# Third expert matrix read with four adjoining rows per partition, in a two-layer encoder step

## Chip, cores and metric

One Trainium2 chip, one core. The metric is the device time of one execution in microseconds, the median of several runs. The profile is one further execution, taken by the hardware profiler.

## The reference, cut to what matters

Two layers, each with a mixer and a mixture of experts. 256 prompt tokens and 128 sample tokens go through, all in float32. The part of concern is the experts' hidden layer, for each of 16 experts in each of two layers:

```python
for e in range(N_EXPERTS):                      # 16
    hdn = jax.nn.silu(t @ w1[e]) * (t @ w3[e])  # t: tokens x 1024; w1, w3: 1024 x 512
    y = y + gates[:, e:e + 1] * (hdn @ w2[e])   # w2: 512 x 1024
```

Each token goes to two experts (top-1 group, top-2 in it). The sum over the 512 inner values in `hdn @ w2[e]` may be taken in any order, as long as value and row belong together.

## The kernel before, in words

Each layer's experts are 16 steps of one pipeline. A step gathers up to 72 (layer 0) or 64 (layer 1) rows of its expert, turns them by TensorE, multiplies them with w1 and w3, takes silu and the product, turns the 512 inner values so that they lie along the partitions (four slices of 128), and multiplies them with w2. Each 2 MB matrix is a tile of 128 partitions x 4096 words. For accuracy, ScalarE writes a rounded copy of it (`moe_split_h`, line 1105, `moe_wh`) and VectorE the remainder (`moe_split_l`, line 1110, into `raw_lo` or `moe_wl`); TensorE uses both parts of the weights and of the data (lines 189 and 195, in layer 1 also 1384 to 1388).

SyncE issues the loads (line 777), three for each expert, in the order w1 of e, w3 of e, w2 of e-1, into six slots that are used in turn. A load waits on `w_used`, until TensorE is done with the matrix that held its slot six loads before; so SyncE runs ahead by what the slots allow. GpSimd loads the gathered rows (line 882), ScalarE's queue stores each expert's output (line 1159).

w1 and w3 are read with eight adjoining rows per partition ("o (p k) n"): 8 x 2 KB = 16 KB of one piece for each partition. w2 is read with rows 128 apart ("o (k p) n"): slice k of partition p is row 128 k + p, four runs of 4 KB each. So the inner values are turned in four contiguous slices of 128 columns. There are two forms of that:

- Layer 0, `transpose_hidden`, line 1402: for each expert four transposes of `hid` (72 rows x 128 columns as the stationary operand, which TensorE loads first; the identity moves). They stand in TensorE's order between the expert's successor's w1 product and its w3 product.
- Layer 1, `fold_hidden`, line 1431: the 128 output rows of w1's and w3's products hold two halves that must be added. A product with `fold` (two identities stacked) turns and adds at once: eight products for each expert, 128x128 stationary from `sil_all` or `hid_all`, 64 columns moving. The machine runs each of these float32 products as two weight loads and two matmuls, so 16 pairs. ScalarE's silu of the turned values (line 1186) and VectorE's `hidden_turned` (lines 1280 to 1284) wait for them, and then the w2 product.

Layer 0 has 72 columns of room for each expert and the plain form, layer 1 has 64 and the folding form. A third place that turns (line 1529) belongs to blocks for experts with more tokens than room; the profile shows no instruction of it.

`by_slice(x, n)` (line 919) views a row of n x 128 words as n slices, slice k being the columns k, k+n, k+2n and so on. VectorE uses it in `weigh_rows` (line 928), with n = 8, to bring the token rows into the order of w1's and w3's rows.

Of the kernel before, what the change touches and what calls it, by code (L numbers as in the profile page):

```python
# [29 lines left out]
P = 128  # L30
# [18 lines left out]
KE = DE // P  # L49
# [5 lines left out]
CAP = max(CAPS)  # L55
# [48 lines left out]
def build(nc, A, O):  # L104

    top = ExitStack()
    with top:
# [21 lines left out]
        ps = top.enter_context(nc.psum_tensor("ps", [P, 8, 512], F32))  # L129
# [548 lines left out]
        sil, hid = sil_all[0:CAP], hid_all[0:CAP]  # L678
# [6 lines left out]
        fold = gain[:, 0:CAPS[1]]  # L685
# [43 lines left out]
        BX, BA, BB, BH, BY, BR = 0, 2, 3, 4, 5, 7  # L729
# [21 lines left out]
        def at_least(eng, s, n):  # L751

            if not isinstance(n, int) or n > 0:
                eng.wait_ge(s, n)
# [7 lines left out]

        def w_in_expert(l, name, e):
            w = A[name][l, bass.ds(e, 1)]
            return w.rearrange("o (k p) n -> p (o k) n" if name == "moe_w2" else "o (p k) n -> p (o k) n", p=P)

        def moe_w_view(w, nk):
            return w.rearrange("p (k n) -> p k n", k=nk)


        def moe_sync(sp, l):
            m0, E0, S = M_MOE[l], NE * l, SLOT[l]

            def load(name, e, j, slot):
                if not (isinstance(j, int) and j < 6):
                    sp.wait_ge(w_used, m0 + j - 5)
                sp.dma_start(moe_w_view(w_raw[slot], KE if name == "moe_w2" else KD),
                             w_in_expert(l, name, e)).then_inc(raw_loaded[slot], 16)
# [42 lines left out]
            with sp.If(n_over > 0):  # L821
                with sp.Fori(0, EXTRA) as i:
                    e = sp.value_load(ovt_i[0:1, bass.ds(i, 1)], min_val=0, max_val=NE - 1)
                    row = sp.value_load(ovt_i[0:1, bass.ds(i + EXTRA, 1)], min_val=0, max_val=SLOTS)
                    sp.wait_ge(y_stored, 16 * (E0 + SENT if l else NE))
                    sp.wait_ge(w_used, m0 + 3 * NE)
                    if l:
                        sp.wait_ge(spread, TILES)
                    at_least(sp, s["st"], 16 * i + 16)
                    sp.dma_start(rows[0:cap, 0, :], xrows[bass.ds(row, cap), :]).then_inc(s["x"], 16)  # L830
                    for slot, name in enumerate(("moe_w1", "moe_w3", "moe_w2")):
                        sp.dma_start(moe_w_view(raw[:, slot, :], KE if slot == 2 else KD),
                                     w_in_expert(l, name, e)).then_inc(s["w"], 16)
                    at_least(sp, s["act"], 5 * i + 5)
                    sp.dma_start(yrows[bass.ds(row, cap), :], rows[0:cap, 2, :]).then_inc(s["st"], 16)
                sp.wait_ge(s["st"], 16 * EXTRA + 16)
# [82 lines left out]
        def by_slice(x, n):  # L919

            return x.rearrange("q (p k) -> q k p", k=n)
# [196 lines left out]
        def turned(i):  # L1118
            n = KE * CAPS[1]
            return ps[:, BH, n * i:n * (i + 1)].rearrange("p (k t) -> p k t", k=KE)  # L1120
# [247 lines left out]
        def moe_tensor(pe, l):  # L1368
# [29 lines left out]
            def transpose_hidden(e):  # L1398
                pe.wait_ge(hid_done, E0 + e + 1)
                at_least(pe, hl_ready, E0 + e)  # L1400
                for k in range(KE):
                    last = nc.tensor.transpose(ps[:, BH, k * CAP:(k + 1) * CAP], hid[:, k * P:(k + 1) * P],
                                               ident[0:CAP, 0:CAP])
                last.then_inc(hT_done, 1)

# [20 lines left out]
            def fold_hidden(e):  # L1426

                pe.wait_ge(halves, 2 * e + 2)
                for i, x in enumerate((sil_all, hid_all)):
                    for k in range(KE):  # L1430
                        last = nc.tensor.matmul(turned(i)[:, k], x[:, k * P:(k + 1) * P], fold, start=True, stop=True)
                last.then_inc(hT_done, 1)

            def folding_step(e, par, m):
                f = is_first(e)
                pe.wait_ge(xl_ready, E0 + e + 1)
                if not f:
                    pe.wait_ge(halves, 2 * e - 1)
                product_x(e, par, *([0, 0, 0] if f else [3 * e - 1, 2, 2 if par else 5]), BA).then_inc(w_used, 1)
                if not f:  # L1440
                    pe.wait_ge(halves, 2 * e)
                product_x(e, par, *([1, 1, 1] if f else [3 * e, 0, 3 if par else 0]), BB).then_inc(w_used, 1)
                if f:
                    gather_x(1)
                elif is_last(e):
                    turn_kept(1)
                elif not is_second(e):
                    transpose_x(e + 1, 1 - par)
                if not f:
                    product_y(e - 1, 3 * e + 1, 1, 4 if par else 1)  # L1450
                fold_hidden(e)
                if is_second(e):
                    transpose_x(2, 0)

            def step(e, par, m):
                f = is_first(e)
                pe.wait_ge(xl_ready, E0 + e + 1)
                at_least(pe, silu_done, E0 + e)
                product_x(e, par, *([0, 0, 0] if f else [3 * e - 1, 2, 2 if par else 5]), BA).then_inc(w_used, 1)
                if not f:  # L1460
                    transpose_hidden(e - 1)
                at_least(pe, hid_done, E0 + e)
                product_x(e, par, *([1, 1, 1] if f else [3 * e, 0, 3 if par else 0]), BB).then_inc(w_used, 1)
                if f:
                    gather_x(1)
                elif not is_last(e):
                    transpose_x(e + 1, 1 - par)
                if not f:
                    product_y(e - 1, 3 * e + 1, 1, 4 if par else 1)
# [19 lines left out]
            if not l:  # L1489
                transpose_hidden(NE - 1)  # L1490
                turn_keys_up(pe)
# [7 lines left out]
            if l:  # L1499
# [4 lines left out]
                for t in range(TILES):  # L1504
                    for c in range(2):
                        last = nc.tensor.matmul(ps[:, SPREAD[t][c]], kept_hot[0:cap, 1, t * P:(t + 1) * P].bitcast(F32),
                                                rows[0:cap, 3, c * 512:c * 512 + 512], start=False, stop=True)
# [4 lines left out]
            with pe.If(n_over > 0):  # L1512
                with pe.Fori(0, EXTRA) as i:
                    pe.wait_ge(s["x"], 16 * i + 16)
                    pe.wait_ge(s["st"], 16 * i + 16)
                    for k in range(KD):
                        last = nc.tensor.transpose(ps[:, BY + k // 4, (k % 4) * CAP:(k % 4 + 1) * CAP],
                                                   rows[0:CAP, 0, k * P:(k + 1) * P], ident[0:CAP, 0:CAP])
                    last.then_inc(s["pe"], 1)
                    pe.wait_ge(s["act"], 5 * i + 1)  # L1520
                    pe.wait_ge(s["w"], 48 * i + 48)
                    for bank, slot in ((BY, 0), (BY + 1, 1)):
                        for k in range(KD):
                            last = nc.tensor.matmul(ps[0:cap, bank], rows[:, 1, k * cap:(k + 1) * cap],
                                                    moe_w_view(raw[:, slot], KD)[:, k], start=k == 0, stop=k == KD - 1)
                    last.then_inc(s["pe"], 1)
                    pe.wait_ge(s["hid"], i + 1)
                    for k in range(KE):
                        last = nc.tensor.transpose(ps[:, BY, k * CAP:(k + 1) * CAP], hid[:, k * P:(k + 1) * P],
                                                   ident[0:CAP, 0:CAP])  # L1530
                    last.then_inc(s["pe"], 1)
                    pe.wait_ge(s["act"], 5 * i + 4)
                    for c in range(2):
                        for k in range(KE):
                            last = nc.tensor.matmul(ps[0:cap, BY + c], rows[:, 3, k * cap:(k + 1) * cap],
                                                    moe_w_view(raw[:, 2], KE)[:, k, c * 512:c * 512 + 512],
                                                    start=k == 0, stop=k == KE - 1)
                    last.then_inc(s["pe"], 1)
# [865 lines left out]
        @block.tensor  # L2404
        def _(pe):
            gm_tensor(pe)
            route_tensor(pe, 0)
            moe_tensor(pe, 0)
            at_tensor(pe)
            route_tensor(pe, 1)  # L2410
            moe_tensor(pe, 1)
# [32 lines left out]
```

## Time and profile before

| what | value |
|---|---|
| time, median of 3 runs | 1062.85 us (1061.85 to 1069.14) |
| the profiled execution's own time | 1060.38 us |
| its span, first to last instruction | 1058.7 us |
| TensorE busy | 1005.1 us (95%) |
| VectorE busy | 761.0 us (72%) |
| ScalarE busy | 604.6 us (57%) |
| HBM read | 260.45 MB |

Layer 0's experts run from about 251 to 548 us, layer 1's from about 768 to 1049 us. Shares of busy time are means over the span; a TensorE that is "busy" has work in its pipeline and isn't always at its peak. PE is TensorE's matmul side, PEld its weight loads, DVE is VectorE, ACT ScalarE, POOL GpSimd and SP SyncE; a q behind the name is that engine's sequencer or queue.

### The profile page before, as it was taken

How to read it: one execution, taken by the hardware profiler on the slowest of the kernel's cores; microseconds unless marked ns; L12 is line 12 of the kernel's file. 1: busy time of each engine (PE TensorE's matmuls, PEld its weight loads, DVE VectorE, ACT ScalarE, POOL GpSimd, SP SyncE). 2: the span in 40 equal slices, each digit the busy share in tenths (PEclk: the TensorE clock that was granted, in tenths of full speed). 3: DMA queues.
4: the chain of work that ended last, by engine and by line, in shares of the span. 5: the costliest groups of instructions: out<-in, count | busy, mean ns of one | idle time of the engine just before them, and what ended most of it. 6: DMA issues, size and time to landing. Idle time of an engine off the chain costs nothing.

```text
span 1058.7 us, 13187 instructions
## 1 busy us (share of the span) xinstructions
PE 1005.1 (95%) x5133; PEld 751.9 (71%) x5133; DVE 761.0 (72%) x651; ACT 604.6 (57%) x499; POOL 84.1 (8%) x110
## 2 busy tenths in 40 slices
PE   4999999999999999999989999989998989999997
PEld 4889998888665666666658775876785667766664
DVE  5456756176689888888835656654858999988897
ACT  5327433234677777777734333435437878888781
POOL 4000000003100000000012021000030000000003
PEclk9999999998999999999999999699998999999999
DMA  9542622683999999999658001403669999999985
GB/s 347 171 169 80 231 80 82 235 366 137 314 379 387 380 401 375 402 383 402 257 154 298 0 6 37 159 1 153 245 263 341 386 403 382 391 408 404 392 358 179
DMA packets 56923, 278.95 MB, mean 263 GB/s; under 512 B 6336, under 2 KB 10848, under 8 KB 48288
## 3 DMA queue, kind: packets, MB, share of 16 engines
q1 hardware_dynamic: 45424, 240.21, 58.9%
q0 software_dynamic: 8992, 29.74, 8.3%
q10 hardware_dynamic: 2464, 8.39, 2.1%
q8 instruction: 31, 0.51, 0.2%
q14 instruction: 12, 0.10, 0.0%
HBM read 260.45 MB, written 18.04 MB: 263 GB/s over the span
## 4 chain that ended last, share of the span: by engine, by line
PE 76%; DVE 11%; DMA 6%; ACT 5%; issue 2%; ACTq 0%; SPq 0%; DVEq 0%
PE ps L189 19%; PE ps L195 10%; PE ps L527 4%; PE ps L581 4%; DMA raw<-in_moe_w_dram 4%; PE ps L1387 4%; PE ps L1384 3%; PE ps L624 3%; DVE raw_lo L1110 3%; PE ps L2112 3%; PE ps L2138 3%; PE ps L587 2%; PE ps L535 2%; PE ps L1419 2%; ACT moe_wh L1105 2%
## 5 line engine op out<-in xcount | busy, mean ns | idle before, releaser
L1110 DVE TENSOR_TENSOR raw_lo<-raw,moe_wh 128x4096 fp32r<-128x4096 f32 x48 | 212.0, 4423 | 35.5 <-ACT moe_wh L1105 35.5
L1110 DVE TENSOR_TENSOR moe_wl<-moe_raw,moe_wh 128x4096 fp32r<-128x4096 f32 x48 | 212.0, 4423 | 35.2 <-ACT moe_wh L1105 35.1
L1105 ACT ACTIVATE moe_wh<-raw 128x4096 fp32r<-128x4096 f32 x48 | 174.0, 3625 | 18.7 <-DMA raw<-in_moe_w_dram 9.5
L1105 ACT ACTIVATE moe_wh<-moe_raw 128x4096 fp32r<-128x4096 f32 x48 | 173.8, 3623 | 13.5 <-DMA moe_raw<-in_moe_w_dram 13.3
L189 PE MATMUL ps<-moe_wh,moe_x 128*72 128x512 f32 x512 | 124.4, 395 | 1.7 <-DVE moe_x L1248 1.5
L189 PEld LDWEIGHTS ps<-moe_wh,moe_x 128*72 128x72 f32 x512 | 71.1, 142 | 45.3 <-DVE moe_x L1248 2.6
L329 DVE TENSOR_TENSOR raw_lo<-raw,gm_wh 128x4096 fp32r<-128x4096 f32 x12 | 53.1, 4426 | 68.2 <-ACT gm_wh L323 65.8
L189 PE MATMUL ps<-moe_wh,moe_hTh 128*72 128x512 f32 (+1 forms) x256 | 81.1, 398 | 3.9 <-DVE moe_hTl L1253 2.1
L189 PE MATMUL ps<-moe_wh,moe_hTl 128*72 128x512 f32 (+1 forms) x256 | 79.8, 393 | 0.0
L1384 PE MATMUL ps<-moe_wh,moe_x 128*128 128x512 f32 x224 | 61.1, 414 | 12.7 <-DVE moe_x L1248 12.7
L323 ACT ACTIVATE gm_wh<-raw 128x4096 fp32r<-128x4096 f32 x11 | 39.9, 3628 | 56.3 <-DMA raw<-in_gm_w_out_dram 28.7
L1384 PEld LDWEIGHTS ps<-moe_wh,moe_x 128*128 128x128 f32 x224 | 42.6, 196 | 22.5 <-issue 9.2
L1151 ACT ACTIVATE moe_rows<-ps 72x1024 f32<-72x1024 f32 (+1 forms) x30 | 30.5, 1017 | 41.4 <-PE ps L195 41.4
L189 PEld LDWEIGHTS ps<-moe_wh,moe_hTl 128*72 128x72 f32 (+1 forms) x256 | 35.4, 138 | 23.7
L189 PEld LDWEIGHTS ps<-moe_wh,moe_hTh 128*72 128x72 f32 (+1 forms) x256 | 33.2, 139 | 22.9 <-DVE moe_hTl L1253 2.5
L527 PE MATMUL ps<-gm_wh,gm_fx 128*128 128x512 f32 x192 | 46.3, 402 | 2.9 <-ACT gm_wh L316 2.9
L1129 ACT ACTIVATE moe_x<-ps 128x576 fp32r<-128x576 f32 (+1 forms) x32 | 20.0, 625 | 50.8 <-PE ps L1376 27.0
L882 POOL DMA_DIRECT2D moe_rows<-moe_xrows x28 | 14.6, 522 | 400.1 <-PE ps L1376 365.9
L581 PE MATMUL ps<-gm_fx,gm_wh 128*128 128x384 f32 x256 | 45.2, 335 | 0.0
L527 PEld LDWEIGHTS ps<-gm_wh,gm_fx 128*128 128x128 f32 x192 | 36.9, 194 | 10.9 <-ACT gm_wh L316 3.2
L581 PEld LDWEIGHTS ps<-gm_fx,gm_wh 128*128 128x128 f32 x256 | 44.3, 188 | 0.1
L195 PE MATMUL ps<-raw_lo,moe_hTh 128*72 128x512 f32 (+1 forms) x144 | 36.2, 393 | 0.0
(411 smaller groups left out, 1723.4 us busy)
## 6 DMA issues: line engine op xcount, KB each, us to landing
raw<-in_moe_w_dram SPq DMA_DIRECT2D x48, 2048.0 KB, 12.5
moe_raw<-in_moe_w_dram SPq DMA_DIRECT2D x48, 2048.0 KB, 12.7
raw<-in_gm_w_in_dram SPq DMA_DIRECT2D x7, 2048.0 KB, 7.9
raw<-in_gm_w_out_dram SPq DMA_DIRECT2D x4, 2048.0 KB, 7.4
moe_yrows<-moe_rows ACTq DMA_DIRECT2D x16, 288.0 KB
moe_rows<-moe_xrows POOLq DMA_DIRECT2D x14, 288.0 KB, 9.5
moe_rows<-moe_xrows POOLq DMA_DIRECT2D x14, 256.0 KB, 8.9
moe_yrows<-moe_rows ACTq DMA_DIRECT2D x14, 256.0 KB
```

Source lines behind the costliest of these rows:

```text
L189: nc.tensor.matmul(out[c], x(t, k), wh[:, k, c * 512:c * 512 + 512], start=start and k == 0 and x is xh, stop=False)
L195: last = nc.tensor.matmul(out[c], xh(t, k), wl[:, k, c * 512:c * 512 + 512], start=False, stop=stop and k == nk - 1)
L323: nc.scalar.activation(w_gm[s][:], raw[:, s, :], ACT.Copy).then_inc(wh_ready, 1)
L329: nc.vector.tensor_tensor(raw_lo[:, s, :], raw[:, s, :], w_gm[s][:].bitcast(F32), ALU.subtract).then_inc(wl_ready, 1)
L527: nc.tensor.matmul(ps[:, 3 * (m % 2) + t], x_rows(x, k, t), wh[:, k], start=k == 0 and x is xth, stop=False)
L581: nc.tensor.matmul(ps[:, u_bank(c), 0:TOK], wh[:, k, i * P:(i + 1) * P], x[:, k], start=k == 0 and x is xth, stop=False)
L624: nc.tensor.matmul(ps[:, 2 * t + c], x_rows(x, 4 * j + k, t), wh[:, k, c * 512:c * 512 + 512], start=j == 0 and k == 0 and x is uth, stop= ...
L1105: nc.scalar.activation(w_hi[hi][:], w_raw[slot], ACT.Copy).then_inc(wh_ready, 1)
L1110: nc.vector.tensor_tensor(w_lo[slot], w_raw[slot], w_hi[hi][:].bitcast(F32), ALU.subtract).then_inc(wl_ready, 1)
L1384: nc.tensor.matmul(ps[:, bank], x[:, k], wh[:, k], start=k == 0, stop=False)
L1387: nc.tensor.matmul(ps[0:cap, bank], xh[:, k], wl[:, k], start=False, stop=False)
L2112: last = nc.tensor.matmul(ps[:, 2 + hp // 2, (hp % 2) * KC:(hp % 2 + 1) * KC], w_uk[:, s, hp * P:(hp + 1) * P], cTs[:, b, s], start=s == 0 ...
```

## The change

w2 is read like w1 and w3: partition p holds the four adjoining rows 4p to 4p+3, one run of 16 KB. Slice k of the tile then holds the rows 4p + k, so the inner values are no longer taken in blocks of 128 columns but by columns four apart: each turn's or fold's stationary operand is read from SBUF with a step of 16 bytes. The count of instructions and the bytes stay the same; the order in which the 512 terms are added changes.

```diff
-            return w.rearrange("o (k p) n -> p (o k) n" if name == "moe_w2" else "o (p k) n -> p (o k) n", p=P)
+            return w.rearrange("o (p k) n -> p (o k) n", p=P)
...
-                    last = nc.tensor.transpose(ps[:, BH, k * CAP:(k + 1) * CAP], hid[:, k * P:(k + 1) * P],
+                    last = nc.tensor.transpose(ps[:, BH, k * CAP:(k + 1) * CAP], by_slice(hid[:], KE)[:, k],
                                                ident[0:CAP, 0:CAP])
...
-                        last = nc.tensor.matmul(turned(i)[:, k], x[:, k * P:(k + 1) * P], fold, start=True, stop=True)
+                        last = nc.tensor.matmul(turned(i)[:, k], by_slice(x, KE)[:, k], fold, start=True, stop=True)
...
-                        last = nc.tensor.transpose(ps[:, BY, k * CAP:(k + 1) * CAP], hid[:, k * P:(k + 1) * P],
+                        last = nc.tensor.transpose(ps[:, BY, k * CAP:(k + 1) * CAP], by_slice(hid[:], KE)[:, k],
                                                    ident[0:CAP, 0:CAP])
```

## Rows read from the trace of the kernel before

**Rows 1.** The page's part 4: the chain that ended last, by engine.

```profile
PE 76%; DVE 11%; DMA 6%; ACT 5%; issue 2%; ACTq 0%; SPq 0%; DVEq 0%
```

**Rows 2.** Chain of layer 0 in order: start us, length us, what ended it.

```profile
353.83 0.25 PE ps L1402 x4
354.08 3.72 PE ps L189 x16
```

**Rows 3.** SyncE's DMA issues of both layers: start us, length us.

```profile
400.71 11.55 SPq L777 DMA_DIRECT2D raw<-in_moe_w_dram  x3
...
435.54 11.55 SPq L777 DMA_DIRECT2D raw<-in_moe_w_dram  x3
...
877.66 9.34 SPq L777 DMA_DIRECT2D raw<-in_moe_w_dram  x3
892.72 9.49 SPq L777 DMA_DIRECT2D moe_raw<-in_moe_w_dram  x3
```

**Rows 4.** Busy time by stretch (both layers): us, five engines, clock, DMA share, GB/s.

```profile
735.00:744.00 9.00, 9.00 (x22) 4.00 (x21) 5.89 (x2) 3.62 (x1) 0.00 (x0) 1.00 1.01 430
747.00:752.00 5.00, 4.54 (x17) 2.27 (x15) 4.87 (x3) 2.66 (x5) 0.00 (x0) 1.00 1.12 419
1012.00:1016.00 4.00, 4.00 (x25) 2.73 (x24) 3.93 (x5) 3.29 (x3) 0.00 (x0) 1.00 1.03 436
1018.00:1024.00 6.00, 6.00 (x36) 4.52 (x35) 5.55 (x3) 5.12 (x5) 0.00 (x0) 1.00 1.02 418
340.00:500.00 160.00, 160.00 (x778) 100.80 (x776) 136.71 (x56) 119.43 (x65) 4.67 (x9) 1.00 1.01 391
860.00:944.00 84.00, 81.80 (x418) 57.47 (x419) 80.93 (x41) 68.42 (x41) 2.54 (x5) 0.98 1.02 394
944.00:1004.00 60.00, 56.50 (x294) 38.83 (x293) 51.96 (x26) 47.61 (x30) 1.53 (x3) 1.00 1.01 400
```

**Rows 5.** Chain of layer 1 in order: start us, length us, what.

```profile
825.54 1.75 PE ps L1431 x16
...
944.00 19.55 DMA raw<-in_moe_w_dram
...
976.64 21.76 DMA raw<-in_moe_w_dram
...
1036.77 1.75 PE ps L1431 x16
```

**Rows 6.** TensorE in layer 1 in order of time, [idle before <-releaser].

```profile
956.05 1.87 PE L1384 MATMUL ps<-moe_wh,moe_x 128*128 128x512 f32 x7 [0.76 <-DVE moe_x L1248]
...
972.49 1.88 PE L1384 MATMUL ps<-moe_wh,moe_x 128*128 128x512 f32 x7 [1.01 <-DVE moe_x L1248]
...
989.56 1.87 PE L1384 MATMUL ps<-moe_wh,moe_x 128*128 128x512 f32 x7 [1.62 <-DVE moe_x L1248]
...
1007.35 1.87 PE L1384 MATMUL ps<-moe_wh,moe_x 128*128 128x512 f32 x7 [2.04 <-DVE moe_x L1248]
```

**Rows 7.** Lines 1402, 1431 and 1477: duration ns min/median/max.

```profile
L1402 PEld LDWEIGHTS ps<-const,moe_hidden x64: 137/141/148, 282.2 to 539.3; 72*128 72x128 f32 x64
...
L1431 PEld LDWEIGHTS ps<-gain,moe_silu x128: 187/192/193, 788.6 to 1037.3; 128*128 128x128 f32 x128
...
L1477 PEld LDWEIGHTS ps<-rt_kept_weight,rt_hot x12: 133/138/138, 842.7 to 1030.9; 128*64 128x64 f32 x12
```

**Rows 8.** VectorE's lines 928 and 1364: duration ns min/median/max.

```profile
L928 DVE TENSOR_TENSOR moe_rows<-h,gain x6: 2035/2046/2289, 226.2 to 753.5; 128x1024 f32<-128x1024 f32 x6
...
L1364 DVE TENSOR_TENSOR h<-h,ps x3: 1220/1222/1223, 1051.4 to 1054.4; 128x1024 f32<-128x1024 f32 x3
```

**Rows 9.** The page's packet count, and two issues of SyncE: start us, length us.

```profile
DMA packets 56923, 278.95 MB, mean 263 GB/s; under 512 B 6336, under 2 KB 10848, under 8 KB 48288
...
731.43 0.54 SPq L777 DMA_DIRECT2D raw<-in_moe_w_dram  x1
...
750.70 0.33 SPq L777 DMA_DIRECT2D raw<-in_moe_w_dram  x1
```

## The prediction

> **What bounds the kernel now.** I read the chain that ended last first: TensorE holds 76% of it, data transfers 6% [rows 1]. A share over two layers hides where each sits, so next comes the chain in order of time. In layer 0 it goes through TensorE only; the four turns of the inner values stand on it as a piece of 0.25 us, directly followed by the next products [rows 2], and there are fifteen such pieces. From 340 to 500 us TensorE is busy for 160.00 of 160.00 us [rows 4], and two experts take 435.54 - 400.71 = 34.8 us, 17.4 each [rows 3]. The transfers are full there too (share 1.01) [rows 4], but no piece of the chain waits for them: layer 0 is TensorE's.
>
> Layer 1 is closer. While TensorE sets the pace an expert takes 892.72 - 877.66 = 15.1 us [rows 3]; it moves three matrices of 2.097 MB, 0.26 MB of rows and 0.26 MB of output, 6.8 MB, and at the 400 GB/s of 944 to 1004 us [rows 4] that is 17.0 us. So TensorE lives for a while on matrices loaded ahead, then they run out: the chain turns to two pieces of transfer, at 944 and 976 us [rows 5], and TensorE idles 0.76, 1.01, 1.62 and 2.04 us ahead of four experts' w1 products [rows 6]. The row names VectorE's work on the tokens; that work stands in VectorE's order behind a matrix whose high part ScalarE could not start before it landed. These 5.4 us are all that faster loads can win there.
>
> **The change part by part.** *The loads.* 32 transfers of w2 go from four runs of 4 KB per partition to one of 16 KB, as w1 and w3 have. The price comes from stretches in which one kind moves nearly alone: 430 GB/s for w1 and w3 at 735 to 744 us, 419 and 418 for w2 at 747 to 752 and 1018 to 1024 [rows 4]. A matrix takes 2.097 MB / 430 = 4.88 us against 2.097 / 419 = 5.00: 0.13 us less. With the 436 GB/s of 1012 to 1016 [rows 4] it is 0.19 us. In layer 0 this is worth nothing, as its chain has no transfer. In layer 1 the last wait [rows 6] is expert 14's; thirteen w2 loads go ahead of its matrices, of which the first went while the mixer still ran, so twelve count: 12 x 0.13 = 1.6 us, at most 12 x 0.19 = 2.3 us. I take 1.7 us, by the two rows that agree. Less than nothing is not expected, since w1 and w3 already move so in the same slots.
>
> The Trainium skill, page "DMA: Bandwidth & Descriptors", section "Why small descriptors are slow (HBM only)", gives each packet about 3 extra cycles and each operation 32 bytes of its own. Worked out from that page, as an estimate, 16 KB in one piece costs 2.3% less than in four, 0.11 us per matrix, and the term would be 1.3 us; the rows' 0.13 us agree with it.
>
> *Issue.* SyncE spends 0.54 us to issue a w2 load and 0.33 us for a w1 load [rows 9]; 0.2 us goes. SyncE stands waiting for TensorE's release of a slot ahead of these issues, and the transfers behind it are queued more than 10 us deep; I cost it at zero. If that queue were empty it would be a gain of 0.2 us per expert at most. No wait is added, and GpSimd's and ScalarE's queues keep their order.
>
> *The stationary operands.* Instructions stay the same in number; the weight loads for turns and folds now read one 4-byte column from every 16 bytes. No row of this trace shows TensorE reading so, hence the bounds. Below, nothing: the same number of columns enters. Above, VectorE: line 928 reads two operands by columns eight apart and takes 2046 ns for 1024 elements, where line 1364 with contiguous operands takes 1222, a ratio of 1.67 [rows 8]. That is 2.0 ns per element with the fixed part in it, so 128 columns cost at most 256 ns.
>
> What is there now? A fold is sixteen pairs in 1.73 to 1.75 us [rows 5], 0.109 us each. Its load shows 192 ns for 128 columns, and line 1477's shows 138 for 64 [rows 7]: 54 ns for 64 columns, 0.84 ns per column, 108 ns for 128. So a fold is bound by its loads and nothing hides them. A turn is quicker: four in 0.25 us [rows 2], 62 ns each, so its load takes at most 0.49 ns per column. And moving columns enter at 3.72 us / 16 / 512 = 0.45 ns [rows 2]. The engine thus reads contiguous columns at about 0.45 ns, and the fold's load uses only half of that pace.
>
> I take the penalty to be a halving of the fast pace: about 0.84 ns per column whenever every column opens a new 16 bytes. Then the fold's loads, already at that pace, cost nothing more, and a turn grows from 62 to 108 ns. In layer 0 that is fifteen pieces x 4 x 46 ns = 2.8 us, all on TensorE's path. I take this value as it is nearest to the rows of the same engine; VectorE's has two strided operands and another clock. If the turn's load stays hidden the term is 0.
>
> *Sum.* 1060.38 (the profiled execution) + 2.8 - 1.7 = 1061.5 us; without the turn's term 1058.7. The profiled execution lies 2.5 us under the median of the runs, 1062.85, and 1.5 under their lowest, so the same sum at the median is 1064. I forecast 1062, no change that this kernel's measurement can tell (about 1%, 10.6 us).
>
> **The rivals.** *The fold's loads slow down too* (slower). If the penalty is a doubling of each load's own time, a pair goes from 0.109 to 0.217 us and a fold from 1.74 to 3.47: 1.73 us for each expert of layer 1. Eight folds are on the chain, the first at 825.54 and the last at 1036.77 us [rows 5]: 13.8 us. The four ahead of the waits of [rows 6] bring 6.9 us, of which 5.4 fall into these waits, which also uses up what the loads would win: 1.5 us. The others (the first experts') lie where VectorE's passes over the matrices set the end. With the turns' 2.8 us it is 18.1 us: 1078.5, at the median 1081. With VectorE's 1.67 instead, 73 ns per pair, it is 8 x 1.17 = 9.3, the four folds' 4.7 us vanish in the waits, and the turns' 0.67 x 62 ns x 60 = 2.5: 11.8 us, 1072. With the upper bound, 256 ns per load, it is 8 x 2.35 + (9.4 - 5.4) + 60 x 194 ns = 18.8 + 4.0 + 11.6 = 34.4 us, 1095. It decides from a fold load of about 0.17 us: then 60 ns x 16 x 8 plus the turns is more than 1%. For it speaks line 928, the only strided read of the trace [rows 8], and that the fold has no cover; against it, that the fold's load runs at half the engine's pace.
>
> The Trainium skill, page "Advanced Engine Details and Errata", section "SBUF Cachelines", speaks against this change: a 16-byte line must be hit at least twice to hide the memory's latency, and another line for each access costs pace. By that rule every column here is penalised. The trace agrees on VectorE (1.67 [rows 8]); no row shows it on TensorE, so the rule carries this rival and its chance, not the forecast.
>
> *The loads win all that is there* (faster). If the full queue gains more than its packets do and all four waits go, with free turns, it is 1060.4 - 5.4 = 1055. To pass 1% it would have to shorten layer 1's start as well, where VectorE sets the end; little speaks for it.
>
> *The runs aren't joined.* If the 16 KB were still cut into 4 KB packets only the turns' 0 to 2.8 us would be left: 1061 to 1066. Against it: 56923 - 48288 = 8635 packets are of 8 KB or more [rows 9], about the 64 x 128 = 8192 runs of w1 and w3.
>
> **How the numbers follow.** Forecast (free folds, turns free or halved in pace; 1058 to 1065): 0.55. Slower by the fold's loads, 1072 to 1095, most likely near 1081: 0.37. All waits gone, 1053 to 1056: 0.06. Runs not joined: 0.02. Half of the gain's case, 0.03, goes beyond 1%, and 0.01 of the slower one's stays within. So faster 0.03, same 0.61, slower 0.36. The range goes from 1055 to 1088: it leaves out the upper end of the slower case (about 0.09) and part of the gain's (about 0.03). The likeliest case alone is 1058 to 1066.
>
> **What would show it.** In the new profile: packets of 8 KB and more rise to about 12,700; 430 GB/s also while w2 moves alone; pairs at line 1431 every 0.11 us and turns at line 1402 every 0.11 us instead of 0.06; an expert of layer 0 at 17.6 us; TensorE's idle time ahead of experts 11 to 14 down by 1.7 us in sum. Wrong it would be with folds of 3 us or more, with a chain in which line 1431's share doubles and the transfers vanish, or with layer 0's experts longer than 17.8 us.

## The result, and the profile after

The changed kernel takes 1084.16 us (median of 4 runs, 1081.61 to 1091.71) against 1064.44 us beside it: ratio 1.0192, 95% interval 1.0127 to 1.0256. Timed again, as the last experiment below, it is 1.0196 (1.0172 to 1.0220), 20.8 us slower. The profiled execution took 1082.94 us with a span of 1081.3, so 22.6 us more span than before. The time lies in the range that I gave, but not where I put it: the rival of the slow folds happened.

I read the new profile in the order of the old one. First the page's chain by engine and the packets, which answer to [rows 1, 9]:

```profile
DMA packets 44636, 278.95 MB, mean 258 GB/s; under 512 B 6337, under 2 KB 10849, under 8 KB 31905
...
PE 87%; DVE 6%; ACT 3%; DMA 2%; issue 1%; ACTq 0%; SPq 0%; DVEq 0%
```

Packets of 8 KB or more are 44636 - 31905 = 12,731: the runs are joined. TensorE went from 76% of the chain to 87%, and the transfers from 6% to 2%: the waits that faster loads were to shorten are gone, but TensorE has filled them with work of its own. Lines 1402 and 1431, which answer to [rows 7], say with what (duration in ns as min/median/max, then first and last start in us):

```profile
L1402 PEld LDWEIGHTS ps<-const,moe_hidden x64: 196/211/221, 282.4 to 542.5; 72*128 72x128 f32 x64
...
L1431 PEld LDWEIGHTS ps<-gain,moe_silu x128: 307/329/330, 791.5 to 1056.6; 128*128 128x128 f32 x128
```

A turn's weight load went from 141 to 211 ns, a fold's from 192 to 329. The last two numbers ahead of the semicolon cut the span into pieces (the last start in line 1431's row is the last load in the first half of the last fold). From the first turn to the last: 260.1 us, before 257.1, so +3.0. From there to the first fold: 249.0 against 249.3. From the first fold to the last: 265.1 against 248.7, +16.4. From there to the end of the span: 24.7 against 21.4, +3.3. Together 22.4; with 0.2 us ahead of the first turn these are the 22.6 of the spans. The chain in order of time, which answers to [rows 2, 5] (start us, length us, what), has one turn of layer 0 and folds of layer 1:

```profile
354.45 0.42 PE ps L1402 x4
...
791.70 3.78 PE ps L1431 x16
810.76 3.62 PE ps L1431 x16
832.33 3.55 PE ps L1431 x16
...
1055.36 3.57 PE ps L1431 x16
```

A fold takes 3.55 us in place of 1.73 to 1.75, 0.222 us for each of its sixteen pairs, and all sixteen folds now stand on the chain. The four waits of [rows 6] are gone; in the view of waits, 780 to 1060 us, TensorE waits ahead of line 1384 for this in all (us in total, times, longest), before and after:

```profile
PE ps L1384 <- DVE moe_x L1248: 12.7, 7, 3.8
```

```profile
PE ps L1384 <- DVE moe_x L1248: 1.4, 1, 1.4
```

SyncE's issues give the pace of an expert, as [rows 3] did:

```profile
402.07 11.70 SPq L777 DMA_DIRECT2D raw<-in_moe_w_dram  x3
...
437.32 11.70 SPq L777 DMA_DIRECT2D raw<-in_moe_w_dram  x3
...
884.69 11.18 SPq L777 DMA_DIRECT2D raw<-in_moe_w_dram  x3
901.59 11.30 SPq L777 DMA_DIRECT2D moe_raw<-in_moe_w_dram  x3
```

In layer 0 two experts take 35.25 us, 17.6 each; in layer 1 one takes 16.9 where it took 15.1. Of the end's 3.3 us, 0.9 is the second half of the last fold (eight pairs at 0.11 us more); the rest lies where TensorE's granted clock is 0.72 on the mean from 1056 to 1068 us, while before it was 1.00 in the stretch after the last fold: the last sixteen products of line 189 take 6.08 us there, before 3.92 (busy time by stretch; of after, then of before):

```profile
1056.00:1068.00 12.00, 10.27 (x34) 6.78 (x34) 8.49 (x9) 0.89 (x2) 3.12 (x4) 0.72 0.63 214
```

```profile
1037.00:1050.00 13.00, 11.21 (x53) 7.22 (x53) 9.60 (x12) 2.41 (x3) 5.39 (x5) 1.00 0.60 203
```

### The profile page after: what moved, and what is told of

Read it like the earlier page. It is cut to its first block, busy times and chain, and to the rows that moved or that the text cites. A ratio compares the mean times of both kernels' runs of the same rounds, so it can differ in the third digit from the quotient of the medians.

```text
span 1081.3 us, 13187 instructions
## 1 busy us (share of the span) xinstructions
PE 1039.5 (96%) x5133; PEld 786.4 (73%) x5133; DVE 760.0 (70%) x651; ACT 604.0 (56%) x499; POOL 85.0 (8%) x110
## 2 busy tenths in 40 slices
DMA packets 44636, 278.95 MB, mean 258 GB/s; under 512 B 6337, under 2 KB 10849, under 8 KB 31905
## 4 chain that ended last, share of the span: by engine, by line
PE 87%; DVE 6%; ACT 3%; DMA 2%; issue 1%; ACTq 0%; SPq 0%; DVEq 0%
PE ps L189 22%; PE ps L195 11%; PE ps L1387 6%; PE ps L1431 5%; PE ps L1384 5%; PE ps L527 4%; PE ps L581 4%; PE ps L624 3%; PE ps L2112 3%; PE ps L2138 3%; PE ps L587 2%; PE ps L535 2%; PE ps L1419 2%; PE ps L631 2%; PE ps L1376 1%
```

## The experiments

The theory from here on: the whole loss is TensorE's, since each strided load takes about twice its own time; 3 us in layer 0, and in layer 1 sixteen folds of 1.82 us less the idle time that they fill. Rivals: the joined loads cost something themselves, or the gain of the loads is hidden behind the slow folds.

**The parts alone, in both layers.** The first kernel has only the new view of w2, the second only the new slices of turns and folds.

```diff
-            return w.rearrange("o (k p) n -> p (o k) n" if name == "moe_w2" else "o (p k) n -> p (o k) n", p=P)
+            return w.rearrange("o (p k) n -> p (o k) n", p=P)
```

> Only w2's reading is changed (one 16 KB run per partition); turns and folds read blocks of 128 columns as before, so values and rows of w2 don't belong together. Theory (the weight loads of TensorE bear the whole loss): span 1055 to 1058.7 us, that is 0 to 3 us under before's 1058.7; folds stay at 1.73 us and turns at 0.25; TensorE's idle time ahead of layer 1's w1 products (12.7 us before, 5.4 of it after 950 us) falls by about 1.7 us. Rival (the longer runs hinder the stream): span over 1062 and more idle time there.

> w2 is read as before (four 4 KB runs), turns and folds read columns four apart as in the change, so values and rows of w2 don't belong together. Theory (weight loads alone): folds 3.55 us, turns 0.42 us, span 1080 to 1084, like the change's 1081.3. Rival (part of the loss is the loads'): span under 1075.

Measured: 1631.03 and 1652.26 us. These whole times tell nothing: the changed values of layer 0 send layer 1's tokens to other experts, and blocks for experts with too many tokens ran, behind the folds, which the kernel before never enters. Up to the last fold the work is the same, and there the parts separate. With the loads alone, turns keep 140 ns per load and 0.25 us on the chain, folds 192 ns; first turn to last 257.2 us, first fold to last 250.8 (before 257.1 and 248.7). With the steps alone, turns have 208 ns and 0.42 us, folds 329 ns; 260.2 and 264.9 us, after's 260.1 and 265.1. So the loss is the steps', up to the last fold, whatever the runs are. The folds' loads, with the loads alone and then with the steps alone:

```profile
L1431 PEld LDWEIGHTS ps<-gain,moe_silu x128: 187/192/192, 790.6 to 1041.4; 128*128 128x128 f32 x128
```

```profile
L1431 PEld LDWEIGHTS ps<-gain,moe_silu x128: 307/329/331, 792.6 to 1057.5; 128*128 128x128 f32 x128
```

**The change in one layer only**, steps and loads together.

```diff
-            return w.rearrange("o (k p) n -> p (o k) n" if name == "moe_w2" else "o (p k) n -> p (o k) n", p=P)
+            return w.rearrange("o (k p) n -> p (o k) n" if name == "moe_w2" and l else "o (p k) n -> p (o k) n", p=P)
...
-                    last = nc.tensor.transpose(ps[:, BH, k * CAP:(k + 1) * CAP], hid[:, k * P:(k + 1) * P],
+                    last = nc.tensor.transpose(ps[:, BH, k * CAP:(k + 1) * CAP], by_slice(hid[:], KE)[:, k],
```

> The change in layer 0 alone (w2's 16 KB runs and the turns by columns four apart); layer 1 as before. Theory: turns 0.42 us instead of 0.25, 16 x 0.17 = 2.7 us more by the end of layer 0, nothing more or less in layer 1: span 1061 to 1062. Rival (the 16 KB runs give something back in layer 0, whose transfers are full too): span 1058.7 or less.

> The change in layer 1 alone; layer 0 as before. Theory: folds 3.55 us, all sixteen on the chain, 16 x 1.82 = 29 us more work on TensorE, of which about 11 us go into idle time that was there: span 1076 to 1079. Rival (my own sum, only eight folds on the chain and 5.4 us absorbed): span 1072 to 1074.

The second is the same for layer 1 ("and not l", and line 1431 by `by_slice`). Measured: layer 0 alone 1068.28 us, ratio 1.0049 (1.0024 to 1.0074), 2.6 to 7.9 us; layer 1 alone 1087.35, 1.0216 (1.0179 to 1.0253), 19.0 to 26.9 us. The turns' stretch is 260.1 us in the first, the folds' stretch 266.6 in the second. So the folds carry most of the loss. The turns' 3.0 us lie at the lower end of the first interval; in its profile the untouched stretch between the last turn and the first fold is 256.2 us instead of 249.3. That stretch is 249.0 to 256.2 us in the profiles of this study, with the turns changed or not, so 7 us there are no sign of the change. Both spans lie above what was expected, 1069.1 and 1084.9 us: the second kernel's untouched stretch is 254.2 us, and its end is 3.4 us longer than before's.

**Two apart instead of four.** Two runs of 8 KB per partition, rows 2p and 2p+1 of each half of w2, so that turns and folds read every second column, 8 bytes apart.

```diff
-            return w.rearrange("o (p k) n -> p (o k) n", p=P)
+            return w.rearrange("o (g p k) n -> p (o g) (k n)" if name == "moe_w2" else "o (p k) n -> p (o k) n", p=P, **({"g": 2} if name == "moe_w2" else {}))
...
-                    last = nc.tensor.transpose(ps[:, BH, k * CAP:(k + 1) * CAP], by_slice(hid[:], KE)[:, k],
+                    last = nc.tensor.transpose(ps[:, BH, k * CAP:(k + 1) * CAP], in_pairs(hid[:])[:, k // 2, k % 2],
...
-                        last = nc.tensor.matmul(turned(i)[:, k], by_slice(x, KE)[:, k], fold, start=True, stop=True)
+                        last = nc.tensor.matmul(turned(i)[:, k], in_pairs(x[:])[:, k // 2, k % 2], fold, start=True, stop=True)
```

> w2 with two runs of 8 KB per partition (rows 256 g + 2 p + k), turns and folds by columns two apart (8 bytes); the result is the reference's. Theory (a load is slowed where each 16 bytes give one column only; two columns out of each are enough): folds 1.73 us, turns 0.25, span 1055 to 1058.7. Rival (any step other than one costs): folds 2.6 to 3.55 us, span 1070 to 1082.

Measured: 1066.14 us, 1.0018 (0.9998 to 1.0038). The folds are nearly free again (1.82 to 1.84 us on the chain). The turns are not: four take 0.42 us on the chain, as at a step of four. So it is not any step that slows a fold, but a turn pays in full at two (the loads, then a piece of the chain):

```profile
L1406 PEld LDWEIGHTS ps<-const,moe_hidden x64: 196/208/221, 285.6 to 545.7; 72*128 72x128 f32 x64
```

```profile
L1435 PEld LDWEIGHTS ps<-gain,moe_silu x128: 194/196/199, 800.0 to 1052.1; 128*128 128x128 f32 x128
```

```profile
357.86 0.42 PE ps L1406 x4
```

**A probe of the steps.** The four slices of each turn and half fold are read with steps of 1, 2, 3 and 4 columns, and 64 columns with steps of 1 and 8 are added; eight small products each with moving columns at steps of 1, 2 and 4 stand in a warm-up.

```diff
-                    for k in range(KE):
-                        last = nc.tensor.matmul(turned(i)[:, k], by_slice(x, KE)[:, k], fold, start=True, stop=True)
+                    nc.tensor.matmul(turned(i)[:, 0], x[:, 0:P], fold, start=True, stop=True)
+                    nc.tensor.matmul(turned(i)[:, 1], x[:, 0:2 * P:2], fold, start=True, stop=True)
+                    nc.tensor.matmul(turned(i)[:, 2], x[:, 0:3 * P:3], fold, start=True, stop=True)
+                    nc.tensor.matmul(turned(i)[:, 3], by_slice(x, KE)[:, 3], fold, start=True, stop=True)
+                    nc.tensor.matmul(turned(i)[0:64, 3], x[:, 0:64], fold, start=True, stop=True)
+                    last = nc.tensor.matmul(turned(i)[0:64, 3], x[:, 0:512:8], fold, start=True, stop=True)
```

> The change's kernel, but each slice of a turn or fold reads another step: one, two, three and four columns with 128 columns each, in the folds also 64 columns with steps one and eight; and 24 extra matmuls of 64 moving columns (rounded float32) with steps one, two and four behind the warm-up. The hidden values are no longer all used, so only the durations count. Theory (a load takes the longer of one column time per column and two per 16-byte line): load durations in the folds 192 ns at steps one and two, about 272 at three (96 lines for 128 columns: 192 column times, 64 x 0.84 ns more), 329 at four, and at 64 columns 138 with step one and 192 with step eight; moving columns as slow with step four as with steps one and two or twice as slow, open. Rival (cost grows with the step): steps two and three between 192 and 329 in even parts, step eight beyond twice.

Its whole time, 1660.88 us, again holds the extra blocks. The loads of the fold (lines 1440 to 1445 in the order of the diff) and of the turn (lines 1410 to 1413, steps 1 to 4):

```profile
L1440 PEld LDWEIGHTS ps<-gain,moe_silu x32: 187/188/192, 797.6 to 1065.9; 128*128 128x128 f32 x32
...
L1441 PEld LDWEIGHTS ps<-gain,moe_silu x32: 196/198/198, 797.8 to 1066.2; 128*128 128x128 f32 x32
...
L1442 PEld LDWEIGHTS ps<-gain,moe_silu x32: 252/258/263, 798.1 to 1066.5; 128*128 128x128 f32 x32
...
L1443 PEld LDWEIGHTS ps<-gain,moe_silu x32: 317/324/330, 798.4 to 1066.8; 128*128 128x128 f32 x32
...
L1444 PEld LDWEIGHTS ps<-gain,moe_silu x32: 132/134/136, 799.0 to 1067.3; 128*64 128x64 f32 x32
...
L1445 PEld LDWEIGHTS ps<-gain,moe_silu x32: 196/206/217, 799.1 to 1067.5; 128*64 128x64 f32 x32
...
L1410 PEld LDWEIGHTS ps<-const,moe_hidden x16: 138/140/143, 286.6 to 545.4; 72*128 72x128 f32 x16
...
L1411 PEld LDWEIGHTS ps<-const,moe_hidden x16: 194/195/204, 286.8 to 545.6; 72*128 72x128 f32 x16
...
L1412 PEld LDWEIGHTS ps<-const,moe_hidden x16: 210/213/213, 286.9 to 545.7; 72*128 72x128 f32 x16
...
L1413 PEld LDWEIGHTS ps<-const,moe_hidden x16: 215/220/220, 287.0 to 545.8; 72*128 72x128 f32 x16
```

The fold's 64 and 128 columns at step 1 differ by 188 - 134 = 54 ns, so 0.84 ns per column and some 80 ns that don't depend on the columns. With these 80 taken off, 128 columns take 108, 118, 178 and 244 ns at steps of 1, 2, 3 and 4, and 64 columns at a step of 8 take 126. In whole 16-byte lines touched per column, these steps are 1/4, 1/2, 3/4, 1 and 1: about 1.9 ns for each line, and never under 0.84 ns per column, gives 108, 122, 182, 243 and 122, close to the theory. Lines of 8 bytes would make a step of 2 as dear as one of 4, lines of 32 bytes a step of 8 twice as dear as one of 4. Of the turn such a sum doesn't hold: its load already goes up by 55 ns at a step of 2 and by 80 at a step of 4. Of the moving columns the probe can't tell: the three groups of eight begin at 250.2, 251.1 and 252.0 us, 0.11 us for a product at a step of 1 and of 2, and the load alone needs that, so a price below it wouldn't show.

**What kind of load it is.** In place of the folds of layer 1, products with 72 rows at steps of 1, 2, 4 and transposes of 128 rows at the same steps, each twice.

```diff
+                    for _ in range(2):
+                        nc.tensor.matmul(one, x[0:CAP, 0:2 * P:2], fold[0:CAP], start=True, stop=True)
...
+                    for _ in range(2):
+                        nc.tensor.transpose(out, x[:, 0:2 * P:2], sq)
```

> A probe in layer 1 in place of each half of the fold, every operation twice: products with 72 rows of the stationary operand at steps of 1, 2 and 4 columns, then transposes of all 128 rows at steps of 1, 2 and 4 (the fold's results are wrong; only the load times of these lines are read). Known so far: a product with 128 rows loads in 188, 197, 324 ns at these steps, a transpose of 72 rows in 140, 195, 220. Theory (the kind of operation sets it: a product's load passes over the columns twice, which hides a step of 2): 72-row products again 188, 197, 324 and 128-row transposes 140, 195, 220. Rival (the number of rows sets it): 72-row products with a step of 2 are slowed as the turn is, and 128-row transposes not.

```profile
L1434 PEld LDWEIGHTS ps<-gain,moe_hidden x64: 192/192/202, 794.4 to 1086.1; 72*128 72x128 f32 x64
```

```profile
L1436 PEld LDWEIGHTS ps<-gain,moe_hidden x64: 196/197/198, 794.9 to 1086.6; 72*128 72x128 f32 x64
```

```profile
L1438 PEld LDWEIGHTS ps<-gain,moe_hidden x64: 308/329/331, 795.3 to 1087.4; 72*128 72x128 f32 x64
```

Products with 72 rows behave as with 128 (192, 197, 329 ns), so a product with the turn's number of rows isn't slowed as the turn is. The transposes of 128 rows settle nothing: outside drops of the clock one takes 0.11 to 0.12 us at every step, and their contiguous loads show 144 to 357 ns in one line.

**The loads without the steps.** The order is made one step earlier: ScalarE's copies of layer 1 and VectorE's product of layer 0 put inner values that lie four apart side by side, and turns and folds read contiguous slices of them. The runs stay joined.

```diff
-                nc.scalar.activation(sil_all[:], ps[:, BA], ACT.Copy).then_inc(halves, 1)
+                nc.scalar.activation(sil_all[:].rearrange("q (k p) -> q k p", k=KE), by_slice(ps[:, BA], KE), ACT.Copy).then_inc(halves, 1)
...
-                nc.vector.tensor_tensor(hid[0:cap], sil[0:cap], ps[0:cap, BB], ALU.mult).then_inc(hid_done, 1)
+                nc.vector.tensor_tensor(in_slices(hid[0:cap]), by_four(sil[0:cap]), by_four(ps[0:cap, BB]), ALU.mult).then_inc(hid_done, 1)
```

> w2 in 16 KB runs as in the change, but the order by columns four apart is made where the hidden values are written: layer 1's copies on ScalarE read PSUM by columns four apart, layer 0's product on VectorE writes its output in slices; turns and folds read blocks of 128 columns again. The result is the reference's. Theory: folds 1.73 us, turns 0.25; ScalarE's copies (587 ns) and VectorE's product (676 ns) grow to at most twice, 0.6 us each; these are covered in layer 0 and in most of layer 1: span 1054 to 1059. Rival (the slow read only moves to the engines that feed the fold, and two copies lie between product and fold): span 1060 to 1070.

Measured: 1063.97 us, 1.0004 (0.9983 to 1.0024). The loads of turns and folds are back at 140 and 192 ns, and with the steps gone the whole loss is gone. ScalarE's copies stay at 587 ns; VectorE's product goes from 675 to 1101, but the chain of layer 0 goes through TensorE alone. The joined runs bring nothing that shows. The profile's span, 1065.8 us, is above the 1054 to 1059 of the theory: 4.9 us of the difference from before lie in the stretch between last turn and first fold, 1.7 between first and last fold.

**The same in layer 1 only**, where changed values send no token elsewhere, so that whole times compare: the joined loads with contiguous folds, then the strided folds with the old loads, then the other way round, w1 and w3 cut into runs of 2 KB (the edit of this last one is shown).

```diff
-            return w.rearrange("o (k p) n -> p (o k) n" if name == "moe_w2" else "o (p k) n -> p (o k) n", p=P)
+            return w.rearrange("o (k p) n -> p (o k) n" if name == "moe_w2" or l else "o (p k) n -> p (o k) n", p=P)
```

> The w2 loads of layer 1 alone go to one run of 16 KB; layer 0, the turns and the folds stay as before (so layer 1 multiplies inner values in an order that is not w2's; the layer's routing is done by then and no work is added). Theory (run length is worth 0.13 us per matrix where the transfers are waited for): TensorE's waits in layer 1 shrink by 1.7 us, from 12.7 to about 11, and the time is 1061 to 1062 against some 1063. Rival (with the queues full the run length is worth nothing): 1063, waits unchanged. Rival (a queue that is issued faster gains more than its packets): 1058 or less.

> The folds of layer 1 alone read columns four apart; all loads stay in 4 KB runs (the values of layer 1 are in an order that is not w2's; no work is added). Theory (the whole loss is TensorE's own: 16 x 1.82 us less the 11 us of idle time that it fills): 1081 to 1088, as with the loads joined in layer 1 (1087), since with TensorE as the only bound no transfer is waited for any more. Rival (the joined runs themselves cost time in layer 1): below 1080. Rival (the joined runs still win something beside the slow folds): above 1089.

> The other way round, and more of it: in layer 1 w1 and w3 too are read in short runs, eight of 2 KB per partition in place of one of 16 KB, while w2 keeps its four of 4 KB (the values of layer 1 follow another order of rows; no work is added). If a packet costs what the stretches of the kernel before showed (0.13 us for three packets more per 16 KB), seven more packets are 0.30 us per matrix, two matrices for each of twelve experts: 7.3 us, so about 1070, and TensorE's waits in layer 1 grow by as much. If run length is worth nothing with the queues full: 1063 and the same waits. If runs of 2 KB meet another limit: 1080 or more.

The joined loads alone: 1065.35 us, 1.0021 (1.0004 to 1.0037), if anything 0.4 to 3.9 us slower. The strided folds alone: 1081.73, 1.0174 (1.0151 to 1.0198), 16.0 to 21.0 us, with waits of 1.4 us as in the changed kernel. The short runs: 1072.82, 1.0087 (1.0057 to 1.0117), 6.1 to 12.4 us. So 2 KB against 16 KB for two matrices is seen, and the 7.3 us that I expected from packets lie in the interval; the waits, though, grew by half a microsecond only, to 13.2, so the time is not lost where I expected it. Two things stand in the trace in its place. The first loads move more slowly: the 9 us that [rows 4] has at 430 GB/s begin 4.9 us after layer 1's first issue, and so placed they show 384 GB/s with the short runs and 421 to 435 in the other kernels (below with the short runs, then with the steps alone in both layers):

```profile
733.55:742.55 9.00, 9.00 (x22) 4.00 (x21) 5.05 (x2) 3.62 (x1) 0.00 (x0) 1.00 1.04 384
```

```profile
739.00:748.00 9.00, 9.00 (x22) 3.99 (x21) 5.94 (x2) 3.62 (x1) 0.00 (x0) 1.00 1.01 428
```

And single issues of SyncE take up to 9.32 us, before 0.54 at most; the longest stands on the chain that ended last:

```profile
957.79 9.32 SPq L777
```

Two drops of the clock, as told below, stand in its profile too. How much of the loss is due to which is not shown.

What became of the gain of the joined loads can be followed in the profile of the first of these three. TensorE's waits in layer 1 did shrink, 7.8 + 2.4 us against 12.7:

```profile
PE ps L1384 <- DVE moe_x L1248: 7.8, 5, 3.1
PE ps L1376 <- DMA moe_rows<-moe_xrows: 2.4, 1, 2.4
```

But first fold to last is 249.0 us, before 248.7. From 935 to 1040 us the four waits of [rows 6] have become two, at every other expert, and the seven matmuls behind them take 2.54 and 2.40 us, not 1.87 (first fence); in just these stretches the granted clock is 0.50, its lower level of 1.2 GHz, and 1.00 ahead of them (second fence):

```profile
957.01 2.54 PE L1384 MATMUL ps<-moe_wh,moe_x 128*128 128x512 f32 x7 [1.32 <-DVE moe_x L1248]
...
990.98 2.40 PE L1384 MATMUL ps<-moe_wh,moe_x 128*128 128x512 f32 x7 [1.63 <-DVE moe_x L1248]
```

```profile
954.60:958.00 3.40, 2.08 (x14) 1.81 (x14) 2.41 (x3) 3.40 (x2) 0.00 (x0) 1.00 0.97 357
958.00:961.40 3.40, 3.40 (x9) 2.00 (x8) 3.40 (x1) 2.08 (x3) 0.00 (x0) 0.50 0.99 424
988.70:992.10 3.40, 1.77 (x11) 1.47 (x11) 2.09 (x3) 3.40 (x2) 0.00 (x0) 1.00 0.97 363
992.10:995.50 3.40, 3.40 (x10) 2.02 (x9) 3.40 (x1) 2.30 (x3) 0.00 (x0) 0.50 1.01 434
```

Two stretches of 3.4 us at half the clock cost up to 2 x 1.7 us, more than the 2.5 us that the waits gave. The other three kernels with joined runs in layer 1 and fast folds (loads alone, two apart, ordered earlier) have two such drops, 34 us apart, each at a wait of 1.2 to 2.4 us, with the expert between them hardly waiting; so has the one with the short runs. The two that load as before in layer 1 (before, and the turns alone) have a wait in each of four experts and no drop from 877 to 1040 us. From first to last fold the four take 249.0 to 252.1 us, these two 248.7 and 247.8. But all this is one profiled execution of each kernel. Over all timed runs the mean granted clock is 0.976 with the joined loads in layer 1 and 0.977 before beside them, 0.977 and 0.976 with two apart, 0.976 and 0.976 with the order made earlier, while two more drops of 3.4 us would be 0.003. So the drops fit the profiles; that the timed runs lost the gain to them is not shown.

**The whole change again**, to see whether its halves, 5.2 and 23.0 us, add up.

> The changed kernel whole, timed in more rounds, since its two halves timed alone gave 5.2 and 23.0 us, 28 together, where the whole change gave 20.4 with an interval of 13.5 to 27.3. If each half costs what its own instructions show (2.9 us for the turns of layer 0, 16 x 1.82 us for the folds less 11 us of idle time: 18), the whole is 21 us and the time 1083 to 1085. Rival (the halves add up as they were timed, so there is a cost that the instructions don't show): 28 us, 1091.

Measured: 1084.55 us, 1.0196 (1.0172 to 1.0220), 18.3 to 23.4 us. The 21 us of the instructions hold, the 28 don't.

## Why the prediction went wrong, point by point

*What bounds the kernel.* Right: layer 0 is TensorE's, and layer 1 had idle time to win. The idle time was more than the 5.4 us of [rows 6]: 12.7 us in the view of waits, of which 11.3 were filled by the slower folds.

*The loads.* -1.7 us was forecast. The waits shrank to 10.2 to 11.7 us in the profiles of the four kernels with joined runs and fast folds, from 12.7 (12.0 in the kernel with the turns alone), about the term, but no time came of it (1.0004, 1.0021). In the profiles drops of the clock stand against it; where the timed runs lost it stays open. And the rows that I priced it by don't bear the price. The 430 against 419 GB/s of [rows 4] are a difference of stretches: in the kernel with joined loads in layer 1 alone, whose timeline is the same up to there, 747 to 752 us shows 410 GB/s with 16 KB runs. Placed at the same distance from layer 1's first issue, this stretch shows 412 to 424 GB/s in the six profiles that read w2 in 4 KB runs there, and 393 to 413 in the eight with longer runs: no sign that w2 moves faster, and not the 430 that were named as a sign.

```profile
747.00:752.00 5.00, 4.68 (x17) 2.27 (x15) 4.86 (x4) 2.52 (x5) 0.00 (x0) 1.00 1.01 410
```

The estimate from the Trainium skill, page "DMA: Bandwidth & Descriptors", section "Why small descriptors are slow (HBM only)", 0.11 us per matrix, is too small for these whole times to show; the shorter waits and the 384 GB/s of the 2 KB runs agree with its direction, w2's stretch does not.

*Issue.* Right that it is worth nothing here: no experiment with shorter issues is faster. The 2 KB runs show that an issue can cost time when it gets long (9.32 us).

*The turns.* The size was right: 0.42 us for four is 0.105 each, where 0.108 was forecast, and 17.6 us for an expert, as forecast. The term was 2.8 us and the stretch grew by 3.0. The reason was not: the penalty was to come "whenever every column opens a new 16 bytes", and with two columns in each 16 bytes four turns take the same 0.42 us. That the size fits is luck.

*The folds: the step that failed.* It reads "I take the penalty to be a halving of the fast pace: about 0.84 ns per column whenever every column opens a new 16 bytes. Then the fold's loads, already at that pace, cost nothing more". The time per column rose in both kinds of load: the turn's from 0.49 to 0.82 ns (0.105 us / 128), the fold's from 0.85 to 1.73 (0.222 us / 128), so the term put at nothing was 1.82 us for each fold. That two loads stand at different paces was taken as a sign that the slower one had room left. It had none at this step, and just enough at a step of 2. The only rows that pointed to it were VectorE's [rows 8], which I set aside as of another engine; their ratio of 1.67 is still under the fold's 2.04, and their two lines differ in more than the step, since line 1364 reads one operand from PSUM. The section "SBUF Cachelines" of the Trainium skill's page "Advanced Engine Details and Errata" was right for the folds: nearly free with two columns in a 16-byte line (197 ns), slow with one (324). For the turn it is too mild: at a step of 2 the load went from 140 to 195 ns and 208 in the kernel with two apart.

*The rival's size.* Its price for a pair, 0.217 us, was measured as 0.222. Its count was not: it has "Eight folds are on the chain", adds four ahead of the waits, and puts the first experts' at nothing. Once each expert has 1.8 us more of TensorE's work, the first experts, where other engines had ended last, are TensorE's too, and all sixteen folds count: from the first fold's first load to the end of the last one's first half, 15.5 folds x 1.82 = 28.2 us, of which 11.3 fall into the waits, leaves 16.9; measured 16.4. That the two misses nearly cancel, four folds too few and 5.9 us of idle time too little, 18.1 against 20.8 us, is luck.

*What would show it.* Of the signs of being wrong, "folds of 3 us or more" and "a chain in which line 1431's share doubles and the transfers vanish" came: 3.55 us, all sixteen folds for eight, and a chain without a transfer from the first fold on. Layer 0's experts stayed under the 17.8 us of the third, at 17.6.

## What to carry to other kernels

Joining short DMA runs moves a stride to some other place; before the loads are priced, ask which instruction reads the stride, and whether anything hides it. A stationary operand without cover is the dearest place: there a step of 16 bytes doubled the time of a float32 product with its load (0.109 to 0.222 us), a step of 8 bytes cost a product's load 5% but a transpose's 39%, and putting the order into a copy that is made anyway cost nothing that could be measured. When work is added to the engine that is almost the bound, count every step in which it becomes the bound, not only those in which it was, and then take off the idle time that it fills.

## What was not expected of the hardware

A product's and a transpose's stationary loads react differently: at a step of 2 columns the product's goes from 188 to 198 ns, the transpose's from 140 to 195. Why was not settled; 72 rows alone do not slow a product so (192, 197, 329 ns).

In the profiles with joined runs TensorE's waits became fewer, and the clock fell: two drops to the lower level, behind waits of 1.2 to 2.4 us, in four kernels of four with joined runs and fast folds (and in the one with short runs, so the long runs as such are not the cause); none behind the waits of 0.76 to 2.04 us of the kernel before. Only the sequence was shown, in one execution of each, and the mean clock of the timed runs shows no such difference; what sets it off was not tried.
